# Modulation pieces moved between groups of the feed-forward blocks, one square sent past an addition, and columns moved in the last pass

## What is computed

```python
def sandwich_in(h, m, sub, p):
    return rms_norm(h, p['norm_pre'][sub]) * (1 + m[:, 3 * sub + 1]) + m[:, 3 * sub]

def sandwich_out(h, y, m, sub, p, weight):
    return h + weight * m[:, 3 * sub + 2] * rms_norm(y, p['norm_post'][sub])

def ffn_sub(h, m, sub, j, p):
    y = swiglu(sandwich_in(h, m, sub, p), p['w_gate'][j], p['w_up'][j], p['w_down'][j])
    return sandwich_out(h, y, m, sub, p, 0.5)
...
mod_x = (jax.nn.silu(c) @ w_mod[l] + b_mod[l]).reshape(bsz, N_MOD, 1, d)
mod_c = (jax.nn.silu(c_ctx) @ w_mod[l] + b_mod[l]).reshape(1, N_MOD, 1, d)
x, xc = trunk_layer(x, xc, mod_x, mod_c, cos, sin, p, l < DEPTH - 1)
```

## Time and profile before

| | us |
|---|---|
| median of 3 runs | 2858.95 |
| lowest and highest run | 2858.63, 2859.75 |
| the profiled execution | 2855.45 |
| its span in the trace | 2853.6 |

### The profile page before, as it was taken

One profiled execution on the slowest core, in us unless ns is written; L12 is line 12 of the kernel. 1 busy time (PEld: TensorE's weight loads), 2 busy tenths in 40 slices (PEclk: granted clock), 3 DMA queues, 4 the chain that ended last, 5 costly groups with the idle time before them and its releaser, 6 DMA issues.

```text
span 2853.6 us, 44747 instructions
## 1 busy us (share of the span) xinstructions
PE 2746.5 (96%) x17138; PEld 2626.1 (92%) x17138; DVE 1975.8 (69%) x3396; ACT 1106.0 (39%) x1932; POOL 804.4 (28%) x619
## 2 busy tenths in 40 slices
PE   6999999999999999999999999999999998999998
PEld 5999999998978899999999999999988878899998
DVE  4776888677445778989886888778666447753434
ACT  3312224353453552324244333324453545522234
POOL 3700313250042375312224822313150024400002
PEclk8999999999999999999999999999999999999999
DMA  7454443452221352443525433443452412553333
GB/s 236 139 152 131 133 127 97 141 151 70 73 83 34 105 162 77 127 136 89 149 77 160 152 107 104 140 134 89 141 145 66 128 30 89 146 140 97 89 94 114
DMA packets 468352, 332.26 MB, mean 116 GB/s; under 512 B 36150, under 2 KB 419484, under 8 KB 467628
## 3 DMA queue, kind: packets, MB, share of 16 engines
q1 hardware_dynamic: 459568, 304.65, 37.2%
q10 hardware_dynamic: 8572, 24.74, 2.4%
HBM read 312.11 MB, written 17.22 MB: 115 GB/s over the span
## 4 chain that ended last, share of the span: by engine, by line
PE 76%; DVE 11%; ACT 4%; issue 4%; POOL 3%; DMA 2%; SPq 0%; ACTq 0%; DVEq 0%; POOLq 0%
PE ps L2432 22%; PE ps L2434 22%; PE ps L2433 22%; DVE wsp L1695 2%; ACT wsp L1100 2%; POOL scr L871 2%; PE ps L2957 2%; DVE macc L1739 2%; PE ps L2932 1%; PE ps L2933 1%; DVE hn L1804 1%; PE ps L2944 1%; POOL wsp L881 1%; ACT hn L1161 1%; DMA raw<-in_ffn_w_gate 1%
## 5 line engine op out<-in xcount | busy, mean ns | idle before, releaser
L2432 PE MATMUL ps<-hn,wsp 128*128 128x384 f32 (+1 forms) x2400 | 775.4, 323 | 22.2 <-DVE wsp L1695 7.9
L2433 PE MATMUL ps<-hn,wsp 128*128 128x384 f32 (+1 forms) x2400 | 767.2, 320 | 0.0
L2434 PE MATMUL ps<-hn,wsp 128*128 128x384 f32 (+1 forms) x2400 | 766.8, 320 | 0.0
L1695 DVE TENSOR_TENSOR wsp<-raw,wsp 128x1024 fp32r<-128x1024 f32 (+3 forms) x304 | 343.9, 1132 | 308.9 <-ACT wsp L1100 307.5
L1100 ACT ACTIVATE wsp<-raw 128x1024 fp32r<-128x1024 f32 (+2 forms) x344 | 320.7, 932 | 468.0 <-PE ps L2434 288.2
L2432 PEld LDWEIGHTS ps<-hn,wsp 128*128 128x128 f32 x2400 | 452.5, 189 | 37.2 <-DVE wsp L1695 8.7
L2432 PE MATMUL ps<-aT,wsp 128*128 128x384 f32 (+1 forms) x1344 | 440.4, 328 | 13.4 <-DVE wsp L1695 5.9
L2433 PEld LDWEIGHTS ps<-hn,wsp 128*128 128x128 f32 x2400 | 452.7, 189 | 0.0
L2434 PEld LDWEIGHTS ps<-hn,wsp 128*128 128x128 f32 x2400 | 452.6, 189 | 0.0
L2433 PE MATMUL ps<-aT,wsp 128*128 128x384 f32 (+1 forms) x1344 | 434.6, 323 | 0.0
L2434 PE MATMUL ps<-aT,wsp 128*128 128x384 f32 (+1 forms) x1344 | 434.5, 323 | 0.0
(11 more groups left out here) (311 smaller groups left out, 4763.2 us busy)
## 6 DMA issues: line engine op xcount, KB each, us to landing
modw<-in_w_mod SPq DMA_DIRECT2D x144, 512.0 KB, 3.9
raw<-in_ffn_w_gate SPq DMA_DIRECT2D x188, 256.0 KB, 3.4
raw<-in_ffn_w_up SPq DMA_DIRECT2D x188, 256.0 KB, 4.1
raw<-in_ffn_w_down SPq DMA_DIRECT2D x96, 256.0 KB, 3.1
raw<-in_ffn_w_down SPq DMA_DIRECT2D x128, 192.0 KB, 2.9
raw<-in_w_in SPq DMA_DIRECT2D x96, 256.0 KB, 3.1
raw<-in_w_out SPq DMA_DIRECT2D x64, 256.0 KB, 3.2
spill<-xT ACTq DMA_DIRECT2D x4, 3072.0 KB, 11.5
```

The lines of the kernel that those rows point to most:

```text
L1695: dve.tensor_tensor(wsp[:, t % 2, 1, at], raw[:, t % RAW, at], wsp[:, t % 2, 0, at].bitcast(F32), ALU.subtract).then_inc(wlo_done, 1)
L2432: pe.matmul(dst, w(0), x(0), start=first, stop=False)
L2433: pe.matmul(dst, w(0), x(1), start=False, stop=False)
L2434: return pe.matmul(dst, w(1), x(0), start=False, stop=last)
```

## The change

It has three parts. The total of pieces (256) and of piece instructions stays.

**A, the table.** In (0, 0), (0, 1) and (1, 0) the UP phase of group 0 has no pieces any more (8 before). In (0, 0) group 1's UP phase takes 34 instead of 26. (0, 1) has 64 instead of 72. (1, 0) gets a table of its own: group 2's UP phase has 20 instead of 10, group 3's 14 instead of 8; its sum is 80 instead of 72, (1, 1) is as before.

**B, one square.** For n = 0 of each norm before a sub-block but the first, the eighth square goes to pair2[0] and from there straight into TensorE's mean as a second sum. GpSimd adds one square less, and TensorE has six such products instead of three (four instead of two in the last). That is five places.

**C, the last pass.** ScalarE makes the first two high parts ahead of the squares in the FFNs too. VectorE computes the columns of an FFN after the second step of the last pass instead of ahead of it. In mixers both are as they were.

```diff
+def single(l, sub, post, n, k): return (l, sub) != (0, 0) and not post and n == 0 and k == KD - 1
...
 MOD_AT = {
-    (0, 0): {(0, UP): [2, 2, 2, 2, 0, 0], (0, DOWN): [0, 2, 2, 2, 2, 2, 2, 2], (1, UP): [2, 4, 2, 2, 2, 4, 2, 4, 2, 2],
+    (0, 0): {(0, DOWN): [0, 2, 2, 2, 2, 2, 2, 2], (1, UP): [2, 4, 4, 4, 4, 4, 4, 2, 4, 2],
...
-    (0, 1): {(0, UP): [2, 2, 2, 2, 0, 0], (0, DOWN): [0, 0, 0, 2, 2, 2, 2, 0], (1, UP): [2, 2, 2, 2, 2],
...
+    (0, 1): {(0, DOWN): [0, 0, 0, 2, 2, 2, 2, 0], (1, UP): [2, 2, 2, 2, 2], (1, DOWN): [2, 2, 2, 2, 2, 2, 2, 0],
+             (2, UP): [2, 2, 2, 2, 2], (2, DOWN): [2, 2, 2, 2, 2, 2, 2, 0], (3, UP): [2, 2, 2, 2, 0, 0, 0]},
+    (1, 0): {(0, DOWN): [0, 0, 0, 2, 2, 2, 2, 0], (1, UP): [2, 2, 2, 2, 2], (1, DOWN): [2, 2, 2, 2, 2, 2, 2, 0],
+             (2, UP): [4, 4, 4, 4, 4], (2, DOWN): [2, 2, 2, 2, 2, 2, 2, 0], (3, UP): [2, 4, 4, 4, 0, 0, 0]},
...
-MOD_AT[1, 0] = MOD_AT[0, 1]
...
-                if k == 0:
+                if k == 0 or single(l, sub, post, n, k):
                     return
...
+                elif single(l, sub, post, n, k):
+                    dst = pair2[0]
...
                 for k in range(KD):
-                    if late is not None and k < 2:
+                    if k < 2:
                         next_hi(last_tile0(l, sub) + k, last_width(l, sub))
                     square(l, sub, 1, 0, k)
-                    if late is None or k >= 2:
+                    if k >= 2:
                         next_hi(last_tile0(l, sub) + k, last_width(l, sub))
...
+            def next_columns(l, sub):
+
+                columns(l, sub, 2)
+                if has_next(after(l, sub)):
+                    columns(*after(l, sub), 0)
+                    columns(*after(l, sub), 1)
+
...
                     next_lo(t0 + dt, last_width(l, sub))
+                    if late is None and dt == 1:
+                        next_columns(l, sub)
...
-                    columns(l, sub, 2)
-                    if has_next(after(l, sub)):
-                        columns(*after(l, sub), 0)
-                        columns(*after(l, sub), 1)
+                    if late is not None:
+                        next_columns(l, sub)
...
+                if single(l, sub, post, n, KD - 1):
+                    pe.wait_ge(sq_done, SQ_AT[l, sub, post, n, KD - 1] + 1)
+                    sums.append(pair2[0])
```

More of the change, by code:

```diff
@@ L400, in paired, with last_add @@
 def paired(l, sub, post, n, k): return (l, sub) != (0, 0) and not post and n == 1 and k >= KD - 2
-ADD_AT = {at: i for i, at in enumerate(at for at in sorted(SQ_AT, key=SQ_AT.get) if at[-1] > 0 and not paired(*at))}
-def last_add(l, sub, post, n): return ADD_AT[l, sub, post, n, KD - 1 - 2 * paired(l, sub, post, n, KD - 1)]
+def single(l, sub, post, n, k): return (l, sub) != (0, 0) and not post and n == 0 and k == KD - 1
+ADD_AT = {at: i for i, at in enumerate(at for at in sorted(SQ_AT, key=SQ_AT.get) if at[-1] > 0 and not paired(*at) and not single(*at))}
+def last_add(l, sub, post, n):
+    at = (l, sub, post, n)
+    return ADD_AT[at + (KD - 1 - 2 * paired(*at, KD - 1) - single(*at, KD - 1),)]
 def pairs_at(l, sub): return 3 * l + sub
@@ L411 @@
 MOD_AT = {
-    (0, 0): {(0, UP): [2, 2, 2, 2, 0, 0], (0, DOWN): [0, 2, 2, 2, 2, 2, 2, 2], (1, UP): [2, 4, 2, 2, 2, 4, 2, 4, 2, 2],
+    (0, 0): {(0, DOWN): [0, 2, 2, 2, 2, 2, 2, 2], (1, UP): [2, 4, 4, 4, 4, 4, 4, 2, 4, 2],
              (1, DOWN): [2, 2, 0, 2, 2, 2, 2, 2], (2, UP): [2, 2, 2, 2, 2], (2, DOWN): [2, 2, 2, 2, 2, 2, 2, 0],
              (3, UP): [2, 2, 2, 2, 2, 0, 0]},
-    (0, 1): {(0, UP): [2, 2, 2, 2, 0, 0], (0, DOWN): [0, 0, 0, 2, 2, 2, 2, 0], (1, UP): [2, 2, 2, 2, 2],
-             (1, DOWN): [2, 2, 2, 2, 2, 2, 2, 0], (2, UP): [2, 2, 2, 2, 2], (2, DOWN): [2, 2, 2, 2, 2, 2, 2, 0],
-             (3, UP): [2, 2, 2, 2, 0, 0, 0]},
+    (0, 1): {(0, DOWN): [0, 0, 0, 2, 2, 2, 2, 0], (1, UP): [2, 2, 2, 2, 2], (1, DOWN): [2, 2, 2, 2, 2, 2, 2, 0],
+             (2, UP): [2, 2, 2, 2, 2], (2, DOWN): [2, 2, 2, 2, 2, 2, 2, 0], (3, UP): [2, 2, 2, 2, 0, 0, 0]},
+    (1, 0): {(0, DOWN): [0, 0, 0, 2, 2, 2, 2, 0], (1, UP): [2, 2, 2, 2, 2], (1, DOWN): [2, 2, 2, 2, 2, 2, 2, 0],
+             (2, UP): [4, 4, 4, 4, 4], (2, DOWN): [2, 2, 2, 2, 2, 2, 2, 0], (3, UP): [2, 4, 4, 4, 0, 0, 0]},
     (1, 1): {(0, UP): [2, 2, 2, 2, 0, 0], (1, UP): [2, 2, 2, 2, 0, 0, 0, 0, 0, 0]},
 }
-MOD_AT[1, 0] = MOD_AT[0, 1]
 def streams_of(u): return 1 if u >= MOD_UNITS + 10 else 2
```

## The result

The changed kernel took 2875.51 us (median of 4 runs, 2873.64 to 2882.24) against 2858.79 (4 runs) of the kernel before: ratio 1.006, 95% interval 1.0048 to 1.0072, that is 14 to 21 us slower. The forecast was 2868, +9.2; the sign and the range hold, the size is some 8 us short. Its profiled execution took 2873.84 us with a span of 2872.0.

A forecast was written before the change was run, and what follows sets the result against it. TensorE, busy 96% of the span, was taken to bound the kernel. Terms +18 - 0.6 - 2.75 - 3.5 + 3.9 - 1.5 - 4.3 gave +9.2 us, from 2858.95 to 2868, with a range of 2857 to 2878.

The forecast's parts named there:

- A1: FFN (0, 0), group 1: added pieces make TensorE wait at three turns; +18 us, bounds 14 and 22.
- the walk: Step-by-step timing of group 1, FFN (0, 0): stalls 5.4, 6.6, 6.6 us, up tile 4 at 273.1.
- two pairs going out close together: Group 1, FFN (0, 0): two adjacent pair DMAs would delay the gate tile, adding 1 to 2 us to the sum.
- the first rival: Group 1, FFN (0, 0): pieces fill VectorE's idle time, costing only +1 to +3; total 2852 us, chance 0.12.
- A2: First groups of FFNs (0, 0), (0, 1), (1, 0): fewer pieces gain 0.6, 2.75 and 3.5 us.
- the bound of -1.45: First group of FFN (0, 1): least gain if gate and up products themselves are the limit, against -2.75 taken.
- The half clock in (1, 0): Low clock behind the first group's stall in FFN (1, 0): its removal worth up to 1.7, taken at 0.8 us.
- A3: Later groups of FFN (1, 0), twice the pieces in the sevens: +3.9 us including turns, from +1.5 to +6.
- less in the next as they only shift once: Sevens of FFN (1, 0): two more pieces exceed the slack by 0.6 us in the first, less in the next.
- two take 1.60 us, so that is the extra work of a step: Sevens of FFN (1, 0): two added pieces cost VectorE 1.60 us per step, against a slack of 1.0.
- Part B does nothing: Rival at the norms' means: eighth square as late as the add; sum +13.6, 2872 us, no separate chance.
- FFN (1, 0) binds too: Rival: with four pieces per seven, pairs' DMAs hold next tiles, eight steps lose 1 us more each; 2877 us, chance 0.11.

The follow-up runs named there:

- e10: The kernel before with nothing changed but the new table row of FFN (0, 0): 2876.13 us, ratio 1.0064.
- e3: The changed kernel, but in group 1 SyncE issues the next chunk's tiles ahead of the second step's pairs: 2856.48 us, ratio 0.9994.
- e8: The kernel before with only the last-pass change (part C), tables and eighth square as before: 2856.01 us, ratio 0.9984.
- e6: The changed kernel with the 16 additional pieces of FFN (1, 0) moved into group 2's DOWN phase: 2916.18 us, ratio 1.0196.
- e5: The kernel before with parts B and C and, in group 1, SyncE's tiles ahead of the second step's pairs: 2848.00 us, ratio 0.9958.

## Why the forecast was right, and where it was short

**A1, right.** The walk said stalls of 5.4, 6.6 and 6.6 us; 5.14, 4.30 and 5.22 came, and up tile 4 at 275.78 where the walk had 273.1. VectorE's holes are 6.88 and 7.18 us behind eight instructions as they were 6.98 behind four: they don't take in pieces. The second and third stall are shorter than in the walk because matmuls ran at a granted clock of 0.50 behind the stall before, so that part of the wait was spent in slow outputs. So the walk put 18.6 us into the stalls where 14.7 came, and 1.5 into the clock where three such stretches came; the sum of both is what was forecast (+18 against 18.8, and 18.3 in e10). That two pairs going out close together would hold the gate tile 1 to 2 us longer did not come: the last two went out at 205.03 and 207.69, and the hole was 6.88. That the holes fill, the first rival, was wrong; e3 shows what it would have taken.

**A2, 0.9 us short.** The waits of 2.59 and 2.60 fell to 1.85 each and not to nothing:

```profile
1132.31 0.62 PE L2534 MATMUL ps<-aT,wsp 128*128 128x384 f32 x2 [1.85 <-DVE aT L1922]
...
1661.73 0.63 PE L2534 MATMUL ps<-aT,wsp 128*128 128x384 f32 x2 [1.85 <-DVE aT L1922]
```

The remainder is the path from the last up output through VectorE, ScalarE and VectorE to the activated half, which pieces don't touch. This was the case behind the bound of -1.45, "if the gate and up products themselves are the limit". The stage gained more than that, since the turn that leaves it takes along a wait of 0.31 us behind it: 1.3 us in each of the two FFNs, which the forecast had not counted as a gain. In the first FFN the wait grew from 0.95 to 1.85 as the turn in front went, as forecast. The half clock in (1, 0), of which 0.8 us was to be won, stayed.

**A3, the term that was mis-sized: +2.5 forecast for the sevens, +9.6 measured.** In the traces 2.9 us of that are lost in group 2's sevens, 2.8 at the end of the group, 3.6 in group 3's sevens and the rest between. Two steps of the forecast failed.

The first is "less in the next as they only shift once". In six of the eight steps that take four pieces TensorE waits for VectorE's sums, 0.25 to 1.11 us each. Group 3 shows why, with pieces at their ordinary 0.75 us. VectorE's four pieces there, and TensorE's wait behind them:

```profile
1969.89 3.30 DVE L1744 SCALAR_TENSOR_TENSOR macc<-modw,silc,macc 128x512 f32<-128x512 f32 x4
...
1977.38 0.44 PE L2444 MATMUL ps<-hn,wsp 128*128 128x384 f32 x1 [0.78 <-DVE scr L2044]
```

They take 1.7 us more than two pieces; against a slack of 1.0 that leaves 0.7, and 0.78 came, much as forecast. But ahead of the pieces VectorE had waited 1.80 us for a high part, and ScalarE, which makes it, had waited for TensorE to get through an output. So each seven starts from TensorE's place again, and the excess comes again: 1.11 us in the next.

The second is "two take 1.60 us, so that is the extra work of a step". That holds only while no sum of GpSimd runs at the same time. The group of rows for VectorE's pieces in group 2 of (1, 0), first of the kernel before, 8 instructions at 748 ns:

```profile
L1739 DVE SCALAR_TENSOR_TENSOR macc<-modw,silc,macc 128x512 f32<-128x512 f32 x8 | 6.0, 748 | 0.5
...
L1706 DVE TENSOR_TENSOR wsp<-raw,wsp 128x512 fp32r<-128x512 f32 x20 | 15.6, 778 | 7.1 <-ACT wsp L1120 7.1
```

and of the changed kernel, 15 of 1125 ns on average (nine near 0.75 us, six between 1.6 and 1.8):

```profile
L1744 DVE SCALAR_TENSOR_TENSOR macc<-modw,silc,macc 128x512 f32<-128x512 f32 x15 | 16.9, 1125 | 1.2
...
L1711 DVE TENSOR_TENSOR wsp<-raw,wsp 128x512 fp32r<-128x512 f32 x20 | 16.7, 836 | 3.1 <-ACT wsp L1123 3.1
```

GpSimd formed the same sums in these sevens before the change, but the pieces fell between them. Now they coincide in three sevens of group 2 and in one of group 3. One seven of the changed kernel (the four pieces take 1.78, 1.60, 0.75 and 0.75 us; the second of the two sums ends at 1848.48):

```profile
1845.55 5.20 DVE L1744 SCALAR_TENSOR_TENSOR macc<-modw,silc,macc 128x512 f32<-128x512 f32 x4
...
1845.15 1.62 POOL L953 TENSOR_TENSOR wsum<-wsum,raw 128x512 f32<-128x512 f32 x1
...
1846.74 1.74 POOL L956 TENSOR_TENSOR raw<-raw 128x512 f32<-128x512 f32 x1
...
1854.93 0.44 PE L2444 MATMUL ps<-hn,wsp 128*128 128x384 f32 x1 [0.72 <-DVE scr L2044]
```

VectorE's idle time in front of its low parts fell from 7.1 to 3.1 us in the five sevens, and VectorE was busy for 65.80 of 72 us in that stretch against 55.58 of 68 before. From 1845.55 to the same place in the next seven VectorE has no gap and needs some 15.7 us, where TensorE needs 14.6. The end of the group waits 1.86 us where it waited 0.60 before, with a half clock behind it:

```profile
1900.84 0.44 PE L2444 MATMUL ps<-aT,wsp 128*128 128x384 f32 x1 [1.86 <-DVE aT L2010]
...
1902.00:1905.00 3.00, 3.00 (x11) 3.00 (x11) 2.44 (x4) 0.03 (x1) 0.00 (x0) 0.50 0.01 3
```

The bounds, +1.5 to +6 with the turns, did not hold this either: 10.9. This account is read from two traces, and no run changes it alone. One thing stays open: why pieces and sums coincide. GpSimd's sums wait for low parts that VectorE, being late, makes shortly ahead of its pieces, and in four of these sevens they waited for the up tile's DMA. The tiles go out later too: the gate tile at 1851.18, behind the step's pairs and 5.6 us after its pieces began, where it went out at 1845.18 before the change, 2 us ahead of the pieces. Whether these sevens with the tiles ahead of the pairs would keep sums and pieces apart was not run.

**B and C.** B gained 2.5 us in the traces against 1.5. At four of its five places it did what was forecast, to 0.2 us (-0.5, -0.5 and -0.5, and +0.35 where there had been no wait). At the first it gained 1.3 where 0.5 was forecast: in the kernel before slow matmuls followed the wait of 1.13 us, with a granted clock of 0.69 from 591.5 to 597 us, and with the change it was 1.00 there. The two-sum mean costs 1.47 us of records, as forecast:

```profile
607.76 1.47 PE L2467 MATMUL ps<-cst,scr 128*128 128x1 f32 x12
```

C gained 4.8 us in the traces and 4.6 in the runs of e8, against 4.3 forecast. At the three last passes TensorE no longer waits, and the moved columns are covered. "Part B does nothing" is wrong by the traces: of the four waits of 1.1 us for GpSimd's last add none is left. "FFN (1, 0) binds too" came nearest among the rivals (2877 in its text, 2868 and eight times 1 us by its terms), and its eight steps did lose about 1 us each. In the seven shown above, VectorE's own work held TensorE; the pairs' DMAs are shown to do so in the DOWN phase (e6), and their share in the sevens is the open point of A3.

**The sum.** The forecast fell 9 us short in the traces: 7.1 by A3, 1.9 by stages that the change doesn't touch, 0.9 by A2 and 0.8 by A1, less 1.0 by B and 0.5 by C. That the measured time still lies inside the range, 2.5 us below its upper end, is owed to the bounds of A1 and not to those of A3.

## What to carry to other kernels

A wait in a queue of DMA issues holds everything behind it: before adding a load that waits for a slot, look at which later load is needed first and put that one ahead. An engine's idle time is room for work only if the wait that ends it would end at the same time with more work in front; here it began anew wherever the pieces ended. And a price read from a row holds only while the neighbours keep their places. A piece took 0.75 us in the sevens before the change, between GpSimd's sums, and 1.6 to 1.8 us when the added work brought both together. Take both prices into the bounds, and ask of a small excess whether it comes once or in every round.

## What the runs showed of the hardware

The same stall is followed by a lower clock in one place and not in another. Behind the two waits of 1.85 us in the changed kernel, first (0, 1), then (1, 0), and behind the first two stalls at the turns:

```profile
1133.00:1136.00 3.00, 3.00 (x19) 3.00 (x18) 1.67 (x3) 2.43 (x3) 0.00 (x0) 1.00 0.04 12
...
1663.20:1666.20 3.00, 3.00 (x11) 3.00 (x10) 0.77 (x2) 1.14 (x1) 0.00 (x0) 0.50 0.00 0
...
209.80:212.30 2.50, 2.50 (x9) 2.50 (x9) 0.00 (x0) 0.00 (x0) 0.00 (x0) 0.50 1.06 338
...
233.20:236.00 2.80, 2.80 (x10) 2.80 (x10) 0.00 (x0) 0.00 (x0) 0.00 (x0) 0.50 0.96 293
```

The granted clock was 1.00 behind the first and 0.50 behind the three others, and in the trace of e5 it was 0.50 in (0, 1) too. By how far the products behind it fall back between two traces laid on each other, such a stretch costs TensorE 1.3 to 2.2 us, so a forecast of a stall of 2 us can't be better than that, and two single traces differ by some such stretches. What decides it stays open.

A piece takes twice as long and more beside GpSimd's sums. Of the 392 instructions on the pieces' line (L1739 before, L1744 with the change), none that no work of GpSimd overlaps takes over 0.76 us: 339 before, 370 with the change. All 40 beside the input sums take 1.50 us, and beside the sums of weights 6 before and 14 with the change take 1.6 to 1.85 us (one more in each takes 1.3). Where only the first sum of a chunk overlaps, 6 and 7 of them, it is 0.75 again; why is open. From start to start it is 0.67 us where two streams alternate, 0.85 us in one stream, and 1.43 us beside the input sums.
